# Four units' first halves ahead of the shift, and the shift's last tile multiplied by TensorE, in a two-block kernel on one core

## The chip, the cores and the metric

One core of a Trainium2 chip runs the whole program in one launch. The metric is the device time of one execution in microseconds. Engines are called TensorE (PE in the profile), its weight loads (PEld), VectorE (DVE), ScalarE (ACT), GpSimd (POOL) and SyncE (SP), which issues all loads.

## The reference, cut to what matters

Two blocks are computed over 512 tokens of width 1024 (8 tiles of 128 channels). The part around the change is the beginning of the first block:

```
mod = silu(c) @ w_cond[l] + b_cond[l]
shift_m, scale_m, gate_m, shift_f, scale_f, gate_f = split(mod, 6)
h = rmsnorm(x, g_mix_pre[l]) * (1.0 + scale_m) + shift_m
q, k, v, u = split(h @ w_in[l], ...)
attn = stick_breaking_attention(q, k, v)      # 8 heads of 64
mix = concat([attn, pooling_mixer(u)]) @ w_out[l]
x = x + gate_m * rmsnorm(mix, g_mix_post[l])
```

A gated feed-forward (2816 wide) follows, then the second block with a chunked state-space mixer, a short convolution and another feed-forward. All results are float32.

## The kernel before, in words

**Layout.** Channels lie on the 128 partitions, tokens along the row, so each activation is 8 tiles of 128x512. A weight matrix is cut into units: one unit is a 128-column strip of the output with all 8 tiles of the contraction, 128x1024 float32. SyncE loads it into a ring of four `raw` buffers. ScalarE rounds it to `whi` (`hi`, L1075), GpSimd writes the rest `wlo = raw - whi` (`lo`, L489; in quarters for the first three units), and activations are split in the same way. A unit is three products for each of 8 tiles, high x high, high x low and low x high: 24 matmuls of 512 columns (`unit`, L549, L550, L553).

**Counters.** The order on each engine is written out by hand; engines wait for counting semaphores. SyncE's queue is one order for all loads: a load whose ring slot is taken holds up all behind it.

**The conditioning.** `mod` is a product with a vector. Its weights come as 48 tiles of 128x1024, `cond`, in a ring of four. VectorE multiplies each by its factor and adds it to `macc` (`mod_unit`, L1610 for the first of eight, L1613 for the others); TensorE then sums `macc` over the partitions with one-column matmuls (`mod_first`, L606; `mod_sum`, L598 for the later parts). Two tiles of the scale (8 and 9) are multiplied by TensorE itself (`mod_direct`, L615). Tiles 0 to 7 are the shift, 8 to 15 the scale of the first norm.

**The start.** SyncE loads x, then the 16 tiles, then units 0 to 3. ScalarE squares x (L1082), TensorE sums the squares (L584), ScalarE makes the root. VectorE multiplies x by it (`norm_x`, L1544) between its conditioning tiles. When shift and scale are both there (`mod_ready` 2), VectorE and ScalarE write the high part `h1h` (L1550, L1128), ScalarE the whole (L1134), VectorE the low part `h1l` (L1554). `first_pair` multiplies units q0 and k0 side by side (L625, L628, L632, L637), then follows v0.

**The heads.** Units come in the order q0 k0 v0 q1 k1 v1 u0 q2 k2 v2 u1 q3 k3 v3 u2 u3. For each head TensorE makes the scores (`scores`, L681); VectorE masks them (L1651), ScalarE and VectorE make a soft-plus (L1195 to L1204, L1661, L1665), TensorE adds the later keys (`later_keys`, L691, L695), ScalarE makes weights (L1211), TensorE the product with the values (`values`, L707). `BETWEEN` says which units stand before and behind the later keys of each head. In every head but the last VectorE adds four more conditioning tiles, and the low parts of q and k (`qk_low`, L1704).

**The output and the joints.** `out_first` is the first output unit; the last conditioning part is summed (`mod_sum(5)`), and three more units follow. Then pieces are handled in halves of 256 tokens: ScalarE squares and copies each output piece (`out_piece`, L1253, L1254), VectorE adds the squares and, once the root is there, the residual (`half_x`, L1595, L1590), ScalarE squares the new x (`x_squares`, L1108), TensorE sums those squares between its strips (`x_sum`, L576, placed by `SUMS_OUT`), ScalarE makes the root (`x_rms`) and h2 is formed (`half_h`, L1566, L1578; `split_half`, L1122). The joint between the blocks is built in the same way, with `down_piece` and h3.

## Time and profile before

| | us |
|---|---|
| median of 3 runs | 1733.77 (1731.59 to 1736.16) |
| the profiled execution | 1734.22 |
| its span | 1732.4 |
| TensorE busy | 1692.5 (98%) |
| TensorE's weight loads | 1377.0 (79%) |
| GpSimd busy | 785.0 (45%) |
| VectorE busy | 734.0 (42%) |
| ScalarE busy | 707.8 (41%) |

The span is that of the profiled execution, from its first to its last instruction; 1.8 us lie around it. The mean granted clock of TensorE is 0.989 of full speed. A share is an average over the span: it doesn't tell which engine ends last in a stage. The chain that ended last is TensorE for 92%, VectorE for 4%, loads and ScalarE for 1% each.

### The profile page before, as it was taken

The numbers are of one execution on the slowest core, as the hardware profiler recorded it, in microseconds if no ns is written. First come the engines' busy times: TensorE is split into PE (matmuls) and PEld (weight loads), VectorE is DVE, ScalarE is ACT, GpSimd is POOL, SyncE is SP. The second block draws the span as 40 slices with busy tenths as digits, with TensorE's granted clock in tenths as the row PEclk, the third lists the DMA queues.
The fourth block names the chain that finished last, engine by engine and source line by source line (L and its number), as shares of the span: only waits on it lengthen the run. The fifth ranks groups of instructions, "written<-read, shape, count | busy, mean of one in ns | idle before, by whom it ended". The sixth has DMA issues, their size and how long they took to land.

```text
span 1732.4 us, 22044 instructions
## 1 busy us (share of the span) xinstructions
PE 1692.5 (98%) x8046; PEld 1377.0 (79%) x8046; DVE 734.0 (42%) x1120; ACT 707.8 (41%) x952; POOL 785.0 (45%) x612
## 2 busy tenths in 40 slices
PE   4999999999999999999999999999999999999998
PEld 3777698888888889888888888887888788888887
DVE  4576825111110026567768778676013222222002
ACT  2655536222223345433534545445223544333232
POOL 0533234444446653543434434445444444444763
PEclk8999999999999999999999999999999999999999
DMA  8544312322323323332332232322333222332332
GB/s 314 190 151 157 123 64 71 116 89 97 97 74 87 96 85 122 123 109 86 101 106 99 96 110 94 101 86 85 98 100 132 96 87 95 97 97 72 93 91 73
DMA packets 54132, 184.61 MB, mean 107 GB/s; under 512 B 5904, under 2 KB 8208, under 8 KB 53680
## 3 DMA queue, kind: packets, MB, share of 16 engines
q1 hardware_dynamic: 54064, 183.67, 32.2%
q8 instruction: 46, 0.75, 0.2%
q14 instruction: 22, 0.18, 0.0%
HBM read 179.39 MB, written 4.26 MB: 106 GB/s over the span
## 4 chain that ended last, share of the span: by engine, by line
PE 92%; DVE 4%; ACT 1%; DMA 1%; issue 1%; SPq 0%; DVEq 0%; ACTq 0%
PE PR L549 26%; PE PR L550 26%; PE PR L553 26%; PE PR L563 2%; PE PR L564 2%; PE PR L565 2%; PE AX L947 1%; DMA cond<-wcond 1%; DVE macc L1613 1%; PE AX L681 1%; PE AX L951 1%; PE AX L707 1%; PE AX L936 1%; PE AX L576 1%; PE AX L691 1%
## 5 line engine op out<-in xcount | busy, mean ns | idle before, releaser
L489 POOL TENSOR_TENSOR wlo<-raw,whi 128x512 fp32r<-128x512 f32 (+1 forms) x600 | 778.8, 1322 | 895.9 <-ACT whi L1075 895.9
L1075 ACT ACTIVATE whi<-raw 128x1024 fp32r<-128x1024 f32 x288 | 301.6, 1051 | 151.5 <-PE PR L553 132.4
L549 PE MATMUL PR<-h3h,whi 128*128 128x512 f32 x608 | 245.5, 404 | 0.0
L550 PE MATMUL PR<-h3l,whi 128*128 128x512 f32 x608 | 240.4, 395 | 0.0
L553 PE MATMUL PR<-h3h,wlo 128*128 128x512 f32 x608 | 154.1, 395 | 0.0
L549 PE MATMUL PR<-h4h,whi 128*128 128x512 f32 x351 | 139.4, 397 | 0.0
L550 PE MATMUL PR<-h4l,whi 128*128 128x512 f32 x351 | 138.6, 395 | 0.0
L553 PEld LDWEIGHTS PR<-h3h,wlo 128*128 128x128 f32 x608 | 114.2, 188 | 27.6
L549 PEld LDWEIGHTS PR<-h3h,whi 128*128 128x128 f32 x608 | 114.3, 188 | 26.7 <-issue 1.2
L550 PEld LDWEIGHTS PR<-h3l,whi 128*128 128x128 f32 x608 | 114.4, 188 | 26.4 <-issue 1.0
L549 PE MATMUL PR<-h2h,whi 128*128 128x512 f32 x320 | 126.7, 396 | 0.0
L550 PE MATMUL PR<-h2l,whi 128*128 128x512 f32 x320 | 126.4, 395 | 0.0
L549 PE MATMUL PR<-fh,whi 128*128 128x512 f32 x308 | 121.9, 396 | 0.0
L550 PE MATMUL PR<-fl,whi 128*128 128x512 f32 x308 | 121.7, 395 | 0.0
L1304 ACT ACTIVATE fh<-ff 128x512 f32 (+1 forms) x44 | 27.8, 632 | 197.0 <-DVE ff L1791 98.5
L1781 DVE TENSOR_TENSOR ff<-sg,PR 128x512 f32<-128x512 f32 x22 | 15.2, 689 | 182.3 <-PE PR L553 175.2
L553 PE MATMUL PR<-h4h,wlo 128*128 128x512 f32 x351 | 89.1, 396 | 0.0
L553 PE MATMUL PR<-h2h,wlo 128*128 128x512 f32 x320 | 81.2, 396 | 0.0
L553 PE MATMUL PR<-fh,wlo 128*128 128x512 f32 x308 | 81.0, 396 | 0.0
L549 PEld LDWEIGHTS PR<-h4h,whi 128*128 128x128 f32 x351 | 65.9, 188 | 16.4 <-issue 0.2
L550 PEld LDWEIGHTS PR<-h4l,whi 128*128 128x128 f32 x351 | 66.0, 188 | 15.9 <-issue 0.2
L553 PEld LDWEIGHTS PR<-h4h,wlo 128*128 128x128 f32 x351 | 65.9, 188 | 16.0
(328 smaller groups left out, 2981.7 us busy)
## 6 DMA issues: line engine op xcount, KB each, us to landing
raw<-w SPq DMA_DIRECT2D x224, 512.0 KB, 3.5
cond<-wcond SPq DMA_DIRECT2D x48, 512.0 KB, 4.6
raw<-w SPq DMA_DIRECT2D x32, 384.0 KB, 3.1
raw<-w SPq DMA_DIRECT2D x32, 320.0 KB, 2.9
abc_a<-acum_rows SPq DMA_DIRECT2D x8, 512.0 KB, 4.0
abc_b<-acum_rows SPq DMA_DIRECT2D x8, 512.0 KB, 4.4
x<-xin SPq DMA_DIRECT2D x1, 2048.0 KB, 10.3
x_keep<-x SPq DMA_DIRECT2D x1, 2048.0 KB, 7.3
```

What stands on the lines that cost most here:

```text
L489: ins = pool.tensor_tensor(wlo[:, j, a:a + n], raw[:, j, a:a + n], whi[:, j, a:a + n], ALU.subtract)
L549: pe.matmul(bank, whi[:, j, w], oh[:, k0 + k, :], start=first and i == 0, stop=False)
L550: pe.matmul(bank, whi[:, j, w], ol[:, k0 + k, :], start=False, stop=False)
L553: mm = pe.matmul(bank, wlo[:, j, k * P:(k + 1) * P], oh[:, k0 + k, :], start=False, stop=last and i == n - 1)
L563: pe.matmul(bank[:, c], whi[:, j, w], oh[:, k0 + k, c], start=start, stop=False)
L564: pe.matmul(bank[:, c], whi[:, j, w], ol[:, k0 + k, c], start=False, stop=False)
L565: return pe.matmul(bank[:, c], wlo[:, j, w], oh[:, k0 + k, c], start=False, stop=stop)
L576: mm = pe.matmul(AX[:, 3, HALF[q % 2]], con_("ones"), sqx[:, k, :], start=k == 0, stop=k == KT - 1)
L681: mm = pe.matmul(AXf[:, c:c + T - j * P], ks[r, p % 2, j * P:(j + 1) * P], qs[r, p % 2, j * P:T], start=j != 3 and i == 0, stop=False, ski ...
L691: mm = pe.matmul(AXf[:, c:c + T - j * P], late[:, 2, :], part[:, c:c + T - j * P], start=False, stop=part is spl and j == NCH - 1, skip_gr ...
L1075: act.activation(whi[:, j, :], raw[:, j, :], ACT.Copy).then_inc(hi_ready, 1)
L1304: act.activation(tile(fh, 2 * i + b), ff[:, b, :], ACT.Copy).then_inc(fh_ready, 1)
```

## The change

The first norm's product is split in two: first x times its root and its scale, `xa` (held in `mixh`, `mixl`), without the shift. Units 0 to 3 (q0, k0, v0, q1) are multiplied with `xa`; what the shift adds to them is a constant for each output channel. It is made apart: the shift in a high and a low part is the stationary operand (two columns, `shifts`), the weights of two units are the moving one (256 columns), which gives two rows (`shift_rows`); two tiny matmuls turn them into columns (`shift_columns`), and VectorE and ScalarE add these when they read q0, k0, v0 and q1. Unit 4 (k1) and all later ones use the whole h1, with the shift (`first_whole`).

The scale is loaded and added ahead of the shift, in two halves of four output tiles (pairs of half-wide tiles, `load_scale`, `mod_scale`). After the first half come the first four tiles of `xa` and the first halves (tiles 0 to 3) of units 0 to 3; after the second half come tiles 4 to 7. x is loaded in two pieces, and squared into buffers of its own. The loads of units 0 to 3 stand between those of the scale, ahead of the shift. The shift's tiles come last; of its eight, VectorE adds seven and TensorE multiplies the last by itself (`mod_direct(KT - 1)`).

k1 moves ahead of the scores of head 0, and q1 too; heads 0 and 1 keep one unit each. `mod_sum(5)` moves behind the second output unit. At the joints, squares of x stand ahead of an output piece on ScalarE and VectorE, and `SUMS_OUT` sums them earlier. Buffers are placed anew (h1l beside, `shifts` and `bias` added).

```
-FIRST_COND = (0, 1, 2, 3, 4, 5, 8, 6, 9, 7, 10, 11, 12, 13, 14, 15)
-DIRECT = (8, 9)
-BETWEEN = [("q1", "k1"), ("v1", "u0"), ("q2", "k2"), ("v2", "u1"), ("q3", "k3"), ("v3",), ("u2",), ("u3",)]
+EARLY = 4
+BETWEEN = [("v1",), ("u0",), ("q2", "k2"), ("v2", "u1"), ("q3", "k3"), ("v3",), ("u2",), ("u3",)]
...
-SUMS_OUT = {(1, 7): (0, 1), (2, 2): (2,), (2, 5): (3,), (2, 7): (4,), (3, 0): (5,), (3, 1): (6,), (3, 2): (7,)}
+SUMS_OUT = {(1, 7): (0, 1), (2, 2): (2,), (2, 4): (3,), (2, 5): (4,), (2, 6): (5,), (2, 7): (6,), (3, 0): (7,)}
...
+            def load_scale(e, i):
+
+                at = RING * e + i
+                j = at % RING
+                if at >= RING:
+                    sp.wait_ge(cond_used, at - RING + 1)
+                src = wcond[KT + 2 * i:KT + 2 * i + 2, :, 512 * e:512 * e + 512].rearrange("a p n -> p a n")
+                sp.dma_start(cond[:, j, :].rearrange("p (a n) -> p a n", a=2), src).then_inc(cond_in[j], 16)
...
+            sp.dma_start(x[:, 0:4, :], xin[:, 0:4, :]).then_inc(s_x[0], 16)
+            sp.dma_start(x[:, 4:KT, :], xin[:, 4:KT, :]).then_inc(s_x[1], 16)
+            for i in range(4):
+                load_scale(0, i)
+            load_in(0)
+            load_in(1)
+            for i in range(4):
+                load_scale(1, i)
+            load_in(2)
+            load_in(3)
+            for n in range(KT):
+                load_cond(KT + n, n)
             sp.dma_start(att[:, :, :], atts[:, :, :]).then_inc(s_att, 16)
...
+            def sumsq(ks):
+
+                for k in ks:
+                    pe.wait_ge(sq_ready, k + 1)
+                    mm = pe.matmul(AX[:, 0, :], con_("ones"), mix1[:, k, :], start=k == 0, stop=k == KT - 1)
+                mm.then_inc(sq_used, 1)
...
+            def early_first():
+
+                for u in range(2):
+                    pe.wait_ge(hi_ready, u + 1)
+                    for k in range(4):
+                        pe.wait_ge(*xa_high(k))
+                        early(u, whi, mixh, k, start=k == 0)
+                for k in range(4):
+                    pe.wait_ge(xa_low, k + 1)
+                    for u in range(2):
+                        early(u, whi, mixl, k)
+                for u in range(2):
+                    pe.wait_ge(lo_ready, u + 1)
+                    for k in range(4):
...
+            def early_unit(u, ks, between=None):
+
+                pe.wait_ge(hi_ready, u + 1)
+                for k in ks:
+                    early(u, whi, mixh, k, start=k == 0)
+                    early(u, whi, mixl, k)
+                if between is not None:
+                    between()
+                pe.wait_ge(lo_ready, u + 1)
+                for k in ks:
+                    early(u, wlo, mixh, k, stop=k == KT - 1)
...
+                    for part in (whi, wlo):
+                        mm = pe.matmul(AX[0:2, 3 - u // 2 * 2, 0:2 * P], shifts[:, k, :], part[:, u:u + 2, k * P:(k + 1) * P],
+                                       start=k == 0 and part is whi, stop=k == KT - 1 and part is wlo,
+                                       skip_group_check=True)
+                mm.then_inc(unit_used, 2)
...
+            sumsq(range(KT))
+            mod_part(1, range(4), 4)
+            early_first()
+            early_unit(2, range(4))
+            early_unit(3, range(4), between=lambda: mod_part(1, range(4, KT), 8))
+            early_second()
+            mod_direct(KT - 1)
+            early_unit(2, range(4, KT))
+            early_unit(3, range(4, KT), between=lambda: mod_part(0, range(KT), 15))
+            shift_rows(0)
+            shift_rows(2)
+            shift_columns(0)
...
+            def first_whole(u):
+
+                pe.wait_ge(hi_ready, u + 1)
+                for k in range(KT):
+                    if k == 4:
+                        shift_columns(2)
...
             out_first()
-            mod_sum(5)
             for m in range(1, 4):
                 if m == 2:
+                    mod_sum(5)
                     pe.wait_ge(pooll_ready, 4)
                 if m == 3:
-                    pe.wait_ge(mod_ready, 3)
+                    pe.wait_ge(mod_ready, 4)
...
+            rms(1, sq_used, 1, dst=AX[:, 1, :])
+            act.wait_ge(mod_ready, 1)
+            xa(0)
             hi(0, 4, 0)
+            xa(2)
             hi(0, 4, 1)
+            for k in range(4):
+                xa_whole(k)
+            hi(0, 4, 2)
+            hi(0, 4, 3)
             act.wait_ge(mod_ready, 2)
-            for k in range(KT // 2, KT):
+            for k in range(4, KT):
+                xa(k)
+            for k in range(4, KT):
+                xa_whole(k)
+            act.wait_ge(mod_ready, 3)
+            act.activation(shifts[:, :, 0], mod[:, 0:KT], ACT.Copy).then_inc(shift_ready, 1)
+            for k in range(6):
                 h1_high(k)
-            for k in range(4):
-                full(k)
-            hi(0, 4, 2)
-            for k in range(4, KT):
-                full(k)
+            hi(0, 4, 4)
+            h1_high(6)
...
+            act.wait_ge(bias_ready, 2)
+            act.activation(kh[:, 0, :], PR[:, 1, :], ACT.Identity, bias=bias[:, 1:2]).then_inc(qkvu_ready, 1)
+            for p in range(2):
+                act.wait_ge(q_whole, p + 1)
+                act.activation(qh[:, p, :], pw[:, p * T:(p + 1) * T], ACT.Copy).then_inc(qkvu_ready, 1)
+            act.wait_ge(bias_ready, 4)
+            act.activation(vT[:, :], PR[:, 2, :], ACT.Identity, bias=bias[:, 2:3]).then_inc(qkvu_ready, 1)
+            hi(0, 4, 5)
             act.wait_ge(s_att, 16)
             act.activation(late[:, :, :], att[:, :, :], ACT.Copy).then_inc(late_ready, 1)
-            for u in range(3):
-                in_step(u)
+            hi(0, 4, 6)
+            in_step(4)
...
-            x_squares(0, (3, 4, 5))
-            out_piece(10)
-            x_squares(0, (6, 7))
+            x_squares(0, range(3, KT))
             hi(0, 4, U_GU1 + 2)
             x_rms(0)
-            split_half(0, h2h, (0, 1), shift1)
+            split_half(0, h2h, (0,), shift1)
+            out_piece(10)
+            split_half(0, h2h, (1,), shift1)
...
-            x_squares(2, (5,))
+            x_squares(2, (5, 6, 7))
             down_piece(8)
-            x_squares(2, (6, 7))
...
+            for i in range(4):
+                mod_scale(0, i)
+            dve.wait_ge(s_x[0], 16)
             dve.wait_ge(r_ready, 1)
...
+            for k in range(4):
+                norm_x(k)
+            scale(0)
+            dve.wait_ge(mod_ready, 1)
+            xa(1)
+            xa(3)
+            for k in range(4):
+                xa_lower(k)
+            for i in range(4):
+                mod_scale(1, i)
+            dve.wait_ge(s_x[1], 16)
+            norm_x(4)
+            scale(1)
+            for k in range(5, KT):
+                norm_x(k)
             dve.wait_ge(mod_ready, 2)
-            make_h()
+            mod_unit(KT)
+            for k in range(4, KT):
+                xa_lower(k)
+            for n in range(1, KT - 1):
+                mod_unit(KT + n)
+            dve.wait_ge(msum_done, 3)
+            dve.tensor_scalar(mod[:, 0:KT], PR[:, 3, 0:KT], 1.0, None, ALU.mult).then_inc(mod_ready, 1)
+            dve.wait_ge(shift_ready, 1)
+            dve.wait_ge(mod_ready, 3)
+            dve.tensor_tensor(shifts[:, :, 1], mod[:, 0:KT], shifts[:, :, 0], ALU.subtract).then_inc(shift_ready, 1)
+
...
+            for k in range(3):
+                h1_lower(k)
+            rows(0)
+            h1_lower(3)
+            h1_lower(4)
+            rows(2)
+            h1_lower(5)
+            columns(0)
+            whole_q(0)
+            h1_lower(6)
+            h1_lower(7)
+            dve.wait_ge(qkvu_ready, 1)
+            dve.scalar_tensor_tensor(kl[:, 0, :], PR[:, 1, :], bias[:, 1:2], kh[:, 0, :], ALU.add,
+                                     ALU.subtract).then_inc(qkl_ready, 1)
+            columns(2)
+            whole_q(1)
+            whole_q_low(0)
+            whole_q_low(1)
...
-            half_x(2, mix2, gffn, lambda k: down_piece(8) if k == 6 else None)
+            half_x(2, mix2, gffn)
+            down_piece(8)
```

`load_cond` and `mod_unit` now count by the position in the ring; a tile's load waits until the tile four places before it is taken.

## Rows read from the trace of the kernel before

**Rows 1.** Waits of TensorE over the whole run: line, releaser: us in total, times, longest.

```profile
PE PR L606 <- DVE macc L1613: 9.8, 2, 9.0
...
PE PR L563 <- DVE h2l L1578: 1.3, 2, 0.9
```

**Rows 2.** Timeline of TensorE at the start: start, us, line, count, idle before and releaser.

```profile
12.75 9.29 PE L584 MATMUL AX<-sq,con 128*128 128x512 f32 x16 [7.46 <-ACT sq L1082]
...
21.95 1.95 PE L615 MATMUL PR<-cvec,cond 128*128 128x1 f32 x16
...
40.18 3.57 PE L606 MATMUL PR<-con,macc 128*128 128x1 f32 x16 [8.99 <-DVE macc L1613]
...
45.26 6.38 PE L625 MATMUL PR<-h1h,whi 128*128 128x512 f32 x16 [1.50 <-DVE h1h L1550]
...
64.64 0.44 PE L681 MATMUL AX<-qh,kh 64*128 64x384 f32 x1
```

**Rows 3.** Windows: busy us of each engine, granted clock, DMA share, GB/s.

```profile
10.00:15.00 5.00, 2.25 (x3) 1.18 (x4) 1.29 (x2) 1.31 (x3) 0.00 (x0) 1.00 0.94 386
...
26.00:27.00 1.00, 0.85 (x8) 0.76 (x7) 0.72 (x1) 0.00 (x0) 0.00 (x0) 0.83 0.84 303
...
50.00:51.00 1.00, 1.00 (x4) 0.73 (x3) 0.55 (x1) 1.00 (x2) 0.15 (x1) 0.72 0.00 0
...
218.00:220.00 2.00, 2.00 (x8) 1.81 (x8) 0.68 (x2) 0.00 (x0) 0.00 (x0) 0.50 0.15 59
```

**Rows 4.** The chain that ended last: start, us, engine and line.

```profile
62.84 1.87 PE PR L553 x8
...
83.45 2.30 PE AX L707 x8
...
221.91 0.43 PE PR L549
```

**Rows 5.** Timeline of VectorE, ScalarE and GpSimd at the start.

```profile
13.32 0.75 DVE L1610 TENSOR_SCALAR macc<-cond,cvec 128x1024 f32<-128x1024 f32 x1 [12.09 <-DMA cond<-wcond]
14.46 5.45 DVE L1613 SCALAR_TENSOR_TENSOR macc<-cond,cvec,macc 128x1024 f32<-128x1024 f32 x4 [0.39 <-DMA cond<-wcond]
...
32.87 1.28 DVE L1544 TENSOR_TENSOR xn<-x,AX 128x512 f32<-128x512 f32 x2
...
38.66 1.06 ACT L1075 ACTIVATE whi<-raw 128x1024 fp32r<-128x1024 f32 x1 [15.21 <-DMA raw<-w]
...
39.79 5.91 POOL L489 TENSOR_TENSOR wlo<-raw,whi 128x256 fp32r<-128x256 f32 x8 [39.34 <-ACT whi L1075]
...
44.07 2.93 ACT L1128 ACTIVATE h1h<-xn,mod,amix 128x512 fp32r<-128x512 f32 x4 [3.07 <-DVE amix L1637]
...
50.85 7.20 POOL L489 TENSOR_TENSOR wlo<-raw,whi 128x256 fp32r<-128x256 f32 x6 [5.15 <-ACT whi L1075]
...
51.51 4.13 DVE L1554 TENSOR_TENSOR h1l<-xn,h1h 128x512 fp32r<-128x512 f32 x4 [0.97 <-ACT xn L1134]
```

**Rows 6.** The conditioning tiles' own view, 0 to 60 us.

```profile
DMA to landing us min/median/max: 4.1/5.1/13.3
```

**Rows 7.** Timeline of VectorE in heads 0 to 2.

```profile
82.01 0.69 DVE L1704 SCALAR_TENSOR_TENSOR kl<-PR,kh 128x512 fp32r<-128x512 f32 x1 [1.08 <-ACT kh L1168]
...
90.09 8.20 DVE L1613 SCALAR_TENSOR_TENSOR macc<-cond,cvec,macc 128x1024 f32<-128x1024 f32 x4
101.36 0.99 DVE L1651 TENSOR_TENSOR AX<-AX,att 128x128 f32<-128x128 f32 x3 [3.07 <-PE AX L681]
```

**Rows 8.** Timeline of TensorE and ScalarE around the last conditioning sum.

```profile
216.63 2.52 PE L598 MATMUL PR<-con,macc 128*128 128x1 f32 x16 [1.61 <-DVE macc L1613]
...
227.43 0.60 ACT L1253 ACTIVATE sq<-PR 128x512 f32<-128x512 f32 x1 [5.40 <-PE PR L553]
```

**Rows 9.** Timeline of TensorE at the joint of the blocks.

```profile
641.84 2.75 PE L576 MATMUL AX<-sqx,con 128*128 128x256 f32 x12
645.33 1.13 PE L576 MATMUL AX<-sqx,con 128*128 128x256 f32 x4 [0.74 <-ACT sqx L1108]
```

More of the change, by code:

```diff
@@ L578, in x_sum @@
                     mm.then_inc(sqx_done, 1)
-            def sumsq(first):
-                for k in range(KT):
-                    pe.wait_ge(sq_ready, first + k + 1)
-                    mm = pe.matmul(AX[:, 0, :], con_("ones"), sq[:, k % 2, :], start=k == 0, stop=k == KT - 1)
-                    mm.then_inc(sq_used, 1)
+            def sumsq(ks):
[3 more added lines that the diff above has]
+                mm.then_inc(sq_used, 1)
             def sum_once(n):
@@ new lines, in early_second @@
+            def early_second():
+                for k in range(4, KT):
+                    pe.wait_ge(*xa_high(k))
+                    for u in range(2):
+                        early(u, whi, mixh, k)
+                for u in range(2):
+                    for k in range(4, KT):
+                        early(u, wlo, mixh, k)
+                for k in range(4, KT):
+                    pe.wait_ge(xa_low, k + 1)
+                    for u in range(2):
+                        early(u, whi, mixl, k, stop=k == KT - 1)
@@ L641, in _, with shift_columns @@
+            def shift_columns(u):
+                pe.wait_ge(rows_taken, u // 2 + 1)
+                for n in (u, u + 1):
+                    mm = pe.matmul(AX[:, u // 2 * 3, n:n + 1], pooled[0:2, n * P:(n + 1) * P], con_("ones", 0, 1, rows=2), start=True,
+                                   stop=True, skip_group_check=True)
+                mm.then_inc(bias_done, 1)
             pe.wait_ge(s_vec, 16)
```

267 lines of the change are left out of this document (140 added, 127 removed).

## The prediction

> **What bounds the kernel.** I read the page first: TensorE is busy 98% of the span and the chain that ended last is 92% TensorE. From its first dense matmul on, time can only come from its idle stretches and from stretches at half clock. So I went to the list of its waits: 9.8 us stand at the start and 1.3 at the first joint between blocks, both at places that the change touches [rows 1]. The timeline of the start shows the reader why: the sum of squares is over at 22.0, the first dense matmul comes at 45.26, the scores of head 0 at 64.64 [rows 2]. Before 45.26 the kernel waits for loads, then for VectorE, which adds the conditioning tiles. The granted clock was 1.00 during the sum of squares, fell inside 26 to 27 and came back inside 50 to 51, 5 us after the first dense matmul [rows 3]. A matmul of 512 columns takes 0.234 us at the upper level (1.87 for eight) and 0.43 at the lower [rows 4]; a unit (24 of them) is 5.6 us.
>
> Two units more are moved ahead of the scores (q1, k1 beside q0, k0, v0), so the start breaks even if the scores begin at 64.6 + 11.2 = 75.9. All times of the new order are my estimates, worked out from rows.
>
> **The start, step by step.** (a) Loads: from the first conditioning tile (13.32) to the first weight unit, sixteen transfers later (38.66), each half megabyte took 1.58 us [rows 5]. The new order puts four half-width scale pairs first: the fourth lands at 18.0, or 18.3 with some 0.1 each for rows half as long (bounds 0 and 0.5). VectorE adds a full tile in 1.36 (5.45 for four) [rows 5]; two half-wide operations I put at 1.5: done at 19.9. Four norm products at 0.64 and the small factors: 22.6. ScalarE's first scaled tile (0.73) and first high weight part (1.0) follow [rows 5]: TensorE starts its first dense matmul at 24.3, 21 us earlier than now. The sum of squares, which starts with the first half of x, is over by 16 and is hidden.
>
> (b) Up to the sum of the second half of the scale TensorE has 44 matmuls. It starts at the lower clock: ten at 0.43 and 34 at 0.234 make 12.4, so 36.7 if nothing waits. But VectorE and GpSimd now work side by side: four low parts and eight half-wide adds against the low weight parts. Where they did so before, a 512-wide VectorE operation took 1.03 (4.13 for four) instead of 0.69 [rows 7], and a quarter of a low weight part 1.2 (7.20 for six) instead of 0.74 (5.91 for eight) [rows 5]. With 1.1 for both, unit 1's low part is ready at 33.4 and unit 2's at 37.5; TensorE waits 2.3 and 1.3 there and reaches the sum at 40.4. It is over at 41.4, and VectorE, idle since 36.7 behind that wait, has the second half of the factors at 41.6.
>
> (c) Behind it in VectorE's queue stand three norm products, the first shift tile, four low parts and three more shift tiles: 1.9 + 0.75 + 2.6 + 3 x 1.38 = 9.4, so 51.0. Only then is the ring slot free for the last shift tile, the one that TensorE multiplies itself; SyncE waits for it there, with the loads of units 4 to 7 queued behind (needed only from 70 on: hidden). The shortest landing of such a tile was 4.1 us [rows 6]: it is there at 55.0.
>
> (d) TensorE finishes what it has (28 matmuls, with short waits for the high parts) at 48.7 and idles 6.3 us, since the multiplication stands ahead of the rest in its queue. Before, the clock fell 5 us after the last dense matmul, in spite of one-column matmuls [rows 2, 3]; so I take it as lower from some 53 on.
>
> (e) From 55.0: sixteen one-column matmuls, 3.57 at the lower clock (1.95 at the upper) [rows 2]; twelve dense at 0.43: 63.7; eight at 0.234, sixteen one-column, four dense: 68.5. The row product of the shift is new: 32 matmuls of 256 columns. No row shows one with two output rows; the nearest bounds are a one-column matmul, 0.12 (1.95 for sixteen), and a 512-column one, 0.234: 3.8 or 7.5. I take 3.8, half the columns of the latter. 72.4. Then unit 4 (5.6), two column turns (1.0), waits for ScalarE's high and GpSimd's low part (1.3), and VectorE's corrected q (0.9): the scores start at 81.2. Against 75.9 the start **costs 5.3**: 21 us of lead are spent on waits and half clock. Bounds: -5 (no gap, no lower clock: 10.2 less) and +9.
>
> **Heads 0 and 1** lose a unit of TensorE work each, 11.2 us; VectorE's conditioning tiles there stay. It had 1.1 and 3.1 us idle and drops one low part (0.7) [rows 7]: 6.3 us of debt. The four tiles of head 1 took 8.20, against 5.45 for four without GpSimd beside them [rows 5, 7], and GpSimd now has one unit less there: up to 2.8 comes back. TensorE asks for the result only behind the values product (2.30) [rows 4]. 6.3 - 2.8 - 2.3: I take **+1.0**, bounds 0 and 6.3.
>
> **The sum of the last conditioning part** is moved behind unit 1 of the output. Now TensorE waits 1.61 for it (from 215.0), then sums at falling clock, and unit 1 is over only at 227.4; the clock was 0.50 in 218 to 220 [rows 3, 8]. 12.4 us for 5.6 + 1.95: moved, the tile is there before it is asked for, and 4.9 return. Units 2 and 3 wait for nothing longer than their own work: **-4.9**, bounds -1.6 and -4.9.
>
> **Joints.** In the first, the squares no longer stand behind an output piece: the first product of h2 had waited 0.9 (1.3 in two waits) [rows 1]: **-1.1**, bounds 0 and -1.3. What is late next there is the piece that was put back; it is due with unit 2 of the next stage, and has 0.4 us. In the second, the last two squares came 0.74 after the six before were summed (641.84 + 2.75 = 644.6; 645.33) [rows 9]; that is on the way to h3, for which TensorE stands idle: **-0.8**, bounds 0 and -1.2. Changed tables, buffers and semaphores cost nothing.
>
> Sum: +5.3 + 1.0 - 4.9 - 1.1 - 0.8 = -0.5. The profiled execution took 1734.22 (span 1732.4): 1733.7. It stands 0.45 above the median of 1733.77, so the forecast for the median is **1733.3**. Some 0.3% (5.2 us) is what a measurement of this kernel can tell from no change.
>
> **A rule weighed.** The Trainium skill (SBUF — State Buffer, section on its two separate sides) calls the port pair of VectorE and GpSimd an exclusive lock: the loser fully blocks for the whole instruction. The measured pairs [rows 5, 7] speak against full exclusion: 0.69 + 0.74 would be 1.43 per pair, and 1.03 to 1.2 was measured. By rows alone, full exclusion would lengthen twelve VectorE operations by 0.33 each: 4.0 later, 1737.3. By that rule this is what to expect.
>
> **Rivals.**
> 1. Forecast, 1733.3: chance 0.45.
> 2. The clock stays up through the gap, or comes back at once: 1.6 + 2.3 less, 1729.4. For: it was up during the idle first 12 us. Against: 26 to 27 [rows 3]. 0.15.
> 3. The gap closes: VectorE is quicker in (b) and (c), the last tile lands before 48.7. 10.2 less: 1723.1. For: (c) hangs on one wait of VectorE, and every us that TensorE gains in (b) is gained twice. Against: 4.1 us of landing behind 9.4 of VectorE. 0.12.
> 4. **Slower:** VectorE becomes the bound of heads 0 to 2. Place: the later keys of heads 1 and 2, which need its low part. Price: the debt of 6.3 in full, 5.3 more: 1738.6. It decides from the point where the four tiles keep their 8.20 and the low part comes more than 2.3 late. For: VectorE worked without a pause between heads there except for 1.1 and 3.1. 0.12.
> 5. Full exclusion of the two engines: 1737.3, 0.08.
> 6. The late sum does not do what it should: the clock falls behind unit 1 instead, or the tile is still late: 1738.2, 0.08. Against: sums of the same kind stand between dense work elsewhere without a wait.
>
> Each case carries some 4 us of its own from the unknown prices. Below 1728.6 lie case 3, almost half of 2 and a tail of 1: 0.26. Above 1739 lie half of 4 and parts of 1, 5 and 6: 0.16. The range of 8 in 10: **1725 to 1740**.
>
> **What would show it.** Right: first dense matmul near 24; TensorE waiting for the last shift tile's load some 6 us and the clock at 0.50 behind it; scores of head 0 at 81; VectorE waiting 4 to 5 us for the column sums of the second half scale; no wait and no half clock around the late sum; no wait over 0.3 at h2. Wrong: scores near 76 or earlier (cases 2, 3); low parts of weights ready as fast as alone (b); waits of the later-keys product in heads 1 and 2 above 2 us (case 4). If the start is right and the median is still below 1728, a stage behind the joints changed that I took as equal.

## The result, and the profile of the changed kernel

The changed kernel took 1738.86 us (median of 7 runs, 1736.63 to 1739.41), beside 1734.82 for the kernel before on the same chip (7 runs). The ratio is 1.0024, with an interval of 1.0015 to 1.0034: **slower by 4.1 us**. The forecast was "the same, 1733.3". The median lies inside the range of 1725 to 1740, but the change did something that can be measured, and it went the other way from the forecast. The rivals that end slower (4, 5 and 6) had 0.28 between them, and 0.16 stood for a time above 1739.

The profiled execution has a span of 1736.5 us, against 1732.4 before: the same 4.1. So the trace can be read as a ledger. First the waits of TensorE over the whole run (line, releaser: us in total, times, longest):

```profile
PE PR L626 <- DMA cond<-wcond: 8.9, 1, 8.9
...
PE PR L632 <- ACT whi L1156: 4.7, 1, 4.7
...
PE PR L632 <- POOL wlo L501: 2.5, 1, 2.5
...
PE PR L575 <- DVE h2l L1666: 1.0, 2, 0.6
```

Before, 9.8 us stood before the column sums and 1.3 at h2l [rows 1]. The largest wait is now on a load, in front of the direct multiplication, and it comes in the middle of dense work. TensorE's timeline of the start:

```profile
18.98 1.05 PE L618 MATMUL PR<-con,macc 128*128 128x1 f32 x8
24.72 3.55 PE L632 MATMUL PR<-mixh,whi 128*128 128x512 f32 x8 [4.69 <-ACT whi L1156]
...
33.58 1.19 PE L632 MATMUL PR<-mixh,wlo 128*128 128x512 f32 x4 [2.51 <-POOL wlo L501]
...
40.82 0.95 PE L618 MATMUL PR<-con,macc 128*128 128x1 f32 x8
...
47.05 2.03 PE L632 MATMUL PR<-mixl,whi 128*128 128x512 f32 x8
57.96 3.57 PE L626 MATMUL PR<-cvec,cond 128*128 128x1 f32 x16 [8.88 <-DMA cond<-wcond]
...
67.96 1.84 PE L618 MATMUL PR<-con,macc 128*128 128x1 f32 x16
70.66 0.28 PE L681 MATMUL AX<-whi,shifts 128*2 128x256 f32 x1
...
83.43 0.41 PE L763 MATMUL AX<-qh,kh 64*128 64x384 f32 x1 [0.93 <-ACT late L1330]
```

It is the order that the forecast had, step for step; the scores of head 0 come at 83.43 instead of 64.64 [rows 2], and with two units (11.2) paid off, the start costs 7.6. Why the load came so late is in the timelines of VectorE, GpSimd and SyncE's queue:

```profile
28.41 7.95 DVE L1718 SCALAR_TENSOR_TENSOR macc<-cond,cvec,macc 128x512 f32<-128x512 f32 x7
36.28 0.67 DVE L1730 TENSOR_TENSOR xn<-x,AX 128x512 f32<-128x512 f32 x1
41.80 0.16 DVE L1725 SCALAR_TENSOR_TENSOR amix<-PR,vec 128x4 f32<-128x4 f32 x1 [4.85 <-PE PR L618]
41.88 1.87 DVE L1730 TENSOR_TENSOR xn<-x,AX 128x512 f32<-128x512 f32 x3
43.67 0.75 DVE L1697 TENSOR_SCALAR macc<-cond,cvec 128x1024 f32<-128x1024 f32 x1
44.34 2.74 DVE L1740 SCALAR_TENSOR_TENSOR mixl<-xn,amix,mixh 128x512 fp32r<-128x512 f32 x4
46.99 6.84 DVE L1700 SCALAR_TENSOR_TENSOR macc<-cond,cvec,macc 128x1024 f32<-128x1024 f32 x5
...
24.75 15.38 POOL L501 TENSOR_TENSOR wlo<-raw,whi 128x256 fp32r<-128x256 f32 x14 [24.30 <-ACT whi L1156]
...
29.55 21.85 SPq L389 DMA_DIRECT2D cond<-wcond  x8
51.45 0.43 SPq L434 DMA_DIRECT2D att<-atts  x1
```

SyncE began the issue of the eighth shift tile at 51.1, when VectorE had emptied the slot, and ended it at 51.4; TensorE went on at 57.96. Counted as in [rows 6], from the start of the issue to the landing, the three last shift tiles took (the tiles' own view, 48 to 55 us):

```profile
L389 SPq DMA_DIRECT2D cond<-wcond x3: 328/328/328, 48.3 to 51.1; - x3
DMA to landing us min/median/max: 3.4/4.7/6.8
```

They were issued 1.4 us apart and landed in their order, after 3.4, 4.7 and 6.8 us. VectorE idles for 4.85 us, from 36.9 to 41.8, waiting for the column sum, at a time when the first two shift tiles already lie in the ring: they landed at 32.9 and 35.3. That line turned out to be the most useful one of the trace.

The granted clock, in windows (busy us of PE, PEld, VectorE, ScalarE, GpSimd, then the clock, DMA share, GB/s):

```profile
36.00:37.00 1.00, 1.00 (x4) 0.80 (x3) 0.95 (x2) 0.00 (x0) 1.00 (x2) 0.50 0.88 360
...
64.00:65.00 1.00, 1.00 (x4) 0.71 (x4) 0.00 (x0) 0.00 (x0) 0.00 (x0) 0.50 1.01 414
87.00:88.00 1.00, 1.00 (x4) 0.81 (x3) 0.00 (x0) 0.97 (x2) 1.00 (x2) 0.50 0.94 340
203.00:204.00 1.00, 1.00 (x3) 0.26 (x2) 0.97 (x5) 0.00 (x0) 0.00 (x0) 0.50 1.02 418
230.00:232.00 2.00, 2.00 (x18) 1.90 (x16) 0.00 (x0) 0.00 (x0) 0.00 (x0) 1.00 0.00 0
```

It is at the lower level (1.2 GHz, 0.50) in 21.0 to 27.9 and in 51.8 to 65.4, as forecast, and in three short stretches that were not: 34.7 to 38.1, 85.9 to 89.3 and 201.9 to 205.4. Around the late sum it is 1.00, where it had been 0.50 before [rows 3].

At the very start the windows mislead. The trace has no record of the clock before 14.2 us here and before 16.4 in the kernel before, and a window without a record prints 1.00. The matmuls of the sum of squares tell more: here they start 0.86 us apart from 10.6 to 14.0 and 0.43 apart from 14.5 on, in the kernel before 0.86 apart from 13.7 to 16.3. So TensorE's first work ran at half the pace of what followed, and the reading "1.00 during the sum of squares" [rows 3] holds only for its second part. That the clock was up in the idle first 12 us, as case 2 of the prediction has it, no row shows.

The ledger, by how much later each point comes than before, the two units taken off up to head 1: scores of head 0, +7.6; scores of heads 3 to 5, +9.4; pool map behind head 7 and first output unit, +10.0; first piece behind the late sum, +5.0; first h2 product, +4.8; first gate of the next stage, +5.1; end, +4.1. So: start +7.6, heads +2.4, tail -5.0, joint 1 nothing, joint 2 -1.0.

### The profile page after: what moved, and what is told of

Same layout as the page of the kernel before. It is cut to its first block, busy times and chain, and to the rows that moved or that the text cites. A ratio compares the mean times of both kernels' runs of the same rounds, so it can differ in the third digit from the quotient of the medians.

```text
span 1736.5 us, 22124 instructions
## 1 busy us (share of the span) xinstructions
PE 1697.9 (98%) x8070; PEld 1378.5 (79%) x8070; DVE 746.5 (43%) x1145; ACT 712.3 (41%) x963; POOL 786.6 (45%) x612
## 3 DMA queue, kind: packets, MB, share of 16 engines
q1 hardware_dynamic: 55232, 183.67, 32.9%
## 4 chain that ended last, share of the span: by engine, by line
PE 94%; DVE 3%; ACT 1%; DMA 1%; issue 0%; POOL 0%; SPq 0%; DVEq 0%; POOLq 0%; ACTq 0%
PE PR L561 26%; PE PR L562 26%; PE PR L565 26%; PE PR L575 2%; PE PR L576 2%; PE PR L577 2%; PE AX L1028 1%; PE AX L789 1%; PE AX L763 1%; PE AX L1032 1%; PE AX L773 1%; PE AX L588 1%; PE PR L632 1%; PE AX L777 1%; PE AX L596 1%; PE AX L1017 1%
## 5 line engine op out<-in xcount | busy, mean ns | idle before, releaser
L561 PEld LDWEIGHTS PR<-h4h,whi 128*128 128x128 f32 x351 | 65.9, 188 | 16.4 <-issue 0.2
```

The source lines that it names most:

```text
L561: pe.matmul(bank, whi[:, j, w], oh[:, k0 + k, :], start=first and i == 0, stop=False)
```

## The experiments

All ratios are against the kernel before, which ran beside each group; the changed kernel stands at 1.0024. Where a gain is given in us of time, it is worked out from the ratios. The groups ran on different chips, so a difference of two ratios carries some 2.3 us of doubt: e2, e4 and e6 lie within it or near its edge, and the others that are set against the changed kernel are clear of it. "Head 0" and "head 3" are the starts of these heads' scores: 83.43 and 128.34 in the changed kernel, 64.64 and 118.98 before.

**e1: the direct multiplication behind units 2 and 3.**

```
             early_second()
-            mod_direct(KT - 1)
             early_unit(2, range(4, KT))
-            early_unit(3, range(4, KT), between=lambda: mod_part(0, range(KT), 15))
+            early_unit(3, range(4, KT))
+            mod_direct(KT - 1)
+            mod_part(0, range(KT), 15)
```

> The changed kernel, with the multiplication of the last shift tile moved on TensorE behind the second halves of units 2 and 3 (24 matmuls). Theory S (the loss at the start is TensorE's: it stands at the last tile, 49.0 to 58.0, with 24 matmuls queued behind that need no tile, and does half of them at the lower clock afterwards): the 24 are done at 54.6, the wait shrinks to 3.4 us, scores of head 0 at 76 to 78.5 instead of 83.4, whole time 5 to 7 us below the changed kernel. Rival R (VectorE is the bound of heads 0 to 2 and takes back what the start saves): scores of head 0 as early, but those of head 3 at most 2 us earlier than in the changed kernel (128.4), whole time 0 to 2 us below it.

Ratio 1.0002 (0.9993 to 1.0012): 3.8 us come back, the whole loss. Timeline of TensorE:

```profile
55.76 2.33 PE L626 MATMUL PR<-cvec,cond 128*128 128x1 f32 x16 [1.84 <-DMA cond<-wcond]
57.95 3.55 PE L618 MATMUL PR<-con,macc 128*128 128x1 f32 x16
```

The wait fell from 8.88 to 1.84, head 0 to 76.33, head 3 to 121.22 (7.1 earlier). So the rival fell, since head 3 came earlier by as much as head 0; but the time gained is less than the theory's 5 to 7. Behind head 3 this trace has three stretches of lower clock (166.4, 197.1 and 647.7), the changed kernel's has one. The same work was only put in another order: what cost was a wait with 5.6 us of ready work queued behind it.

**e2: the last tile's load with nothing behind it** (SyncE waits for its landing before it issues the next loads).

```
+            sp.wait_ge(cond_in[RING - 1], 64)
             sp.dma_start(att[:, :, :], atts[:, :, :]).then_inc(s_att, 16)
```

> The changed kernel, with all loads behind the last shift tile held back until that tile has landed. Theory S (the tile landed 7 us after its issue at 51 instead of 4.1, because ten loads issued right behind it share the engines): it lands by 55.5, scores of head 0 at 81, whole time 2 to 3 us below the changed kernel. Rival L (7 us is what a tile costs there, whoever else loads): it lands near 58 again, the time is the same within 0.5 us.

Ratio 1.0017 (1.0007 to 1.0026), head 0 at 82.41. From the start of its issue the tile took 6.1 us to land with no load behind it, while the kernels that kept the loads there (e6, e1, e3, e4, e7 and the changed one) gave 5.1, 5.4, 5.7, 5.7, 6.4 and 6.8. The loads queued behind are not what makes it late: the theory fell. Two things are left open. One is scatter: e4 has the same start as the changed kernel, to the instruction, and its tile took 5.7. The other is what stands in front: in e2 too the two tiles before it, issued 1.4 us apart, took 3.4 and 4.4. Whether the last one queues behind those, no run here tests.

**e3: the gap filled with dense work** (32 matmuls of 512 columns into a bank that nobody reads, ahead of the direct multiplication; they add nothing to the result).

```
             early_second()
+            for k in range(32):
+                pe.matmul(AX[:, 0, :], whi[:, 0, 0:P], mixh[:, k % KT, :], start=True, stop=True, skip_group_check=True)
             mod_direct(KT - 1)
```

> The changed kernel, with 32 dense matmuls into an unused bank put ahead of the multiplication of the last shift tile: they fill 7.5 us of the 8.9 us in which TensorE stood idle, and compute nothing that is used. Theory S (the clock falls in the gap and costs 3.9 us behind it: sixteen one-column matmuls at 3.6 instead of 2.0, twelve dense at 0.43 instead of 0.234): granted clock 1.00 from 50 to 70, scores of head 0 at 79.5, whole time 3.5 to 5.5 us below the changed kernel. Rival C (the clock there costs nothing, since the shift waits for VectorE anyway): the same within 0.5 us.

Ratio 0.9997 (0.9987 to 1.0006): 4.7 us under the changed kernel with more work done. In its trace:

```profile
49.62 7.63 PE L705 MATMUL AX<-mixh,whi 128*128 128x512 f32 x32
57.51 1.95 PE L626 MATMUL PR<-cvec,cond 128*128 128x1 f32 x16 [0.27 <-DMA cond<-wcond]
```

The direct multiplication is back at its 1.95 [rows 2]; the clock stayed at 1.00 until 59.5, then was low for 3.4 us instead of 13.6. Head 0 came at 81.08, where the theory had 79.5: the profiled execution gained only 2.4 us at heads 0 and 3; the ratio gained more. So the gap has two prices: 8.9 us of standing, and a clock that stays low for 7.5 us after it.

**e4: the late sum put back ahead of unit 1.**

```
             out_first()
+            mod_sum(5)
             for m in range(1, 4):
                 if m == 2:
-                    mod_sum(5)
```

> The changed kernel with the last conditioning sum back ahead of the second output unit, as before. Theory S (moving it returned 5.1 us: end of the output unit after it 10.0 us late against before on one side, 4.9 on the other): 4 to 5.5 us above the changed kernel, TensorE waits 1.6 us for VectorE there and the clock falls behind it. Rival T (the gain at that place came from the shifted phase of the work around it, not from the move): within 1.5 us of the changed kernel.

Ratio 1.0040 (1.0027 to 1.0054): 2.8 us more than the changed kernel, less than expected. The profile shows the wait of 1.63 again; the clock did fall, at 227.9 to 231.3, but for 3.4 us instead of 6.8 before (217.8 to 224.6). (The expectation of e9 below says that it did not fall here; that is wrong.)

**e5: VectorE takes the last shift tile.**

```
-            mod_direct(KT - 1)
...
-            early_unit(3, range(4, KT), between=lambda: mod_part(0, range(KT), 15))
+            early_unit(3, range(4, KT), between=lambda: mod_part(0, range(KT), 16))
...
-            for n in range(1, KT - 1):
+            for n in range(1, KT):
```

> VectorE takes the last shift tile as it takes the others, and TensorE's own multiplication of it is gone; the column sum of the shift stays where it is, between the two passes of unit 3. Theory (what costs is the place of TensorE's wait, not who multiplies): the tile lands at 56 to 58, VectorE needs 1.0 to 1.4 us for it, TensorE has meanwhile done the second half of unit 2 and the first pass of unit 3, the sum starts at 57.5 to 59.5 instead of 67.96, and the scores of head 0 come at 74 to 77 instead of 83.4; the time is 3.5 to 5.5 us under the changed kernel's. Rival (TensorE's multiplication itself saves something that VectorE then has to pay): scores of head 0 above 79 and less than 2.5 us gained.

Ratio 0.9989 (0.9979 to 0.9999), 6 us under the changed kernel, a little more than expected, though head 0 at 77.7 is later than the theory's 77. Timelines of VectorE and TensorE:

```profile
58.14 1.28 DVE L1699 SCALAR_TENSOR_TENSOR macc<-cond,cvec,macc 128x1024 f32<-128x1024 f32 x1 [1.48 <-DMA cond<-wcond]
...
59.48 3.57 PE L618 MATMUL PR<-con,macc 128*128 128x1 f32 x16 [4.87 <-DVE macc L1699]
```

This undoes the part of the change that its short description names. The tile landed just as late (58.1), VectorE added it in 1.28, and TensorE had by then done the 4.7 us of work that it otherwise left behind its wait.

**e6: the scale's second column sum 2.9 us earlier** (between the passes of unit 2 instead of unit 3).

```
-            early_unit(2, range(4))
-            early_unit(3, range(4), between=lambda: mod_part(1, range(4, KT), 8))
+            early_unit(2, range(4), between=lambda: mod_part(1, range(4, KT), 8))
+            early_unit(3, range(4))
```

> Only the second half of the scale's column sum moves on TensorE, from between the passes of unit 3 to between those of unit 2, about 2.9 us earlier (VectorE has its operand ready at about 36.3). Theory (the last shift tile waits for its slot, the slot for VectorE, and VectorE for this sum): VectorE's idle stretch of 4.85 us shrinks to 2 to 2.5, the slot comes free 2.5 to 3 us earlier, the direct multiplication starts at 54.5 to 55.5, scores of head 0 at 80 to 81.5, and the time falls by 2 to 3 us against the changed kernel. Rival (the landing is set by the transfers, not by the slot): direct multiplication still at 56.5 or later, time within 1 us of the changed kernel.

Ratio 1.0011 (1.0001 to 1.0020), 2.3 us gained. VectorE's idle stretch fell to 2.08, the direct multiplication came at 53.59, head 0 at 79.72. The direct multiplication came 4.4 earlier: the slot was free 2.7 earlier, as the theory had it, and the other 1.7 are a landing of 5.1 us instead of 6.8.

**e7: VectorE's idle stretch filled.**

```
-            norm_x(4)
-            scale(1)
-            for k in range(5, KT):
+            for k in range(4, KT):
                 norm_x(k)
-            dve.wait_ge(mod_ready, 2)
             mod_unit(KT)
+            mod_unit(KT + 1)
+            scale(1)
+            dve.wait_ge(mod_ready, 2)
+            mod_unit(KT + 2)
+            mod_unit(KT + 3)
             for k in range(4, KT):
                 xa_lower(k)
-            for n in range(1, KT - 1):
+            for n in range(4, KT - 1):
```

> VectorE alone is reordered: the last three normalizations and the first two shift tiles fill its idle stretch ahead of the scale's factors, and the third and fourth shift tile go ahead of the low parts. Theory: VectorE is busy from 36.3 to about 41, frees the slot of the last shift tile at 44.5 to 45.5 instead of 50.6, the tile lands at 49.5 to 51.5, TensorE's idle stretch behind the first two units shrinks from 8.9 us to 0.5 to 2.5, scores of head 0 at 76 to 78.5, the time 4.5 to 7 us under the changed kernel's. Rival (the shift tiles have not landed by 41, or land 7 us after their slot whatever is done): idle stretch above 4 us, time less than 3.5 us under.

Ratio 0.9987 (0.9978 to 0.9997), 6.4 us gained. Timelines of SyncE's queue and of TensorE:

```profile
29.49 15.30 SPq L389 DMA_DIRECT2D cond<-wcond  x8
44.84 0.43 SPq L434 DMA_DIRECT2D att<-atts  x1
...
50.91 2.31 PE L626 MATMUL PR<-cvec,cond 128*128 128x1 f32 x16 [2.08 <-DMA cond<-wcond]
```

The eighth tile was issued at 44.8 instead of 51.4, and head 0 and head 3 moved by 7.4 each. Nothing was taken away; VectorE only did ready work while it waited: its next conditioning tile begins at 38.6 instead of 43.7.

**e8: e7, and the direct multiplication between units 2 and 3.**

```
-            mod_direct(KT - 1)
             early_unit(2, range(4, KT))
-            early_unit(3, range(4, KT), between=lambda: mod_part(0, range(KT), 15))
+            mod_direct(KT - 1)
+            mod_part(0, range(KT), 15)
+            early_unit(3, range(4, KT))
```

> VectorE as in the run before this one, and on TensorE the direct multiplication and the shift's column sum stand between the second halves of unit 2 and unit 3, so that unit 3 covers what the other engines do with the sum. Theory: no wait above 1 us at the direct multiplication, which starts at 51 to 53; shift rows done at 60 to 63; scores of head 0 at 69.5 to 73 instead of 83.4; 8 to 12 us under the changed kernel, 1727 to 1731, so 4 to 8 us under the kernel before. Rival (VectorE then bounds the first heads, and gives back what came earlier): scores of head 0 as said, but head 3 less than 7 us earlier than in the changed kernel, and less than 5 us gained in time.

Ratio 0.9962 (0.9950 to 0.9975): 10.8 us under the changed kernel and 6.6 under the one before. No wait is left at the direct multiplication (52.90). Head 0 at 73.05, head 3 at 119.18, 9.2 earlier: the next heads gave back 1.2. The trace shows a stretch of lower clock at 74.3 to 81.1 that takes 3.1 up to head 1, of which 1.2 are left at head 3.

**e9 and e12: the old start.** e9 is the kernel before with only `mod_sum(5)` moved as in the change; e12 also has the new `SUMS_OUT` and the new orders of squares and pieces at both joints, so that only the start is the old one.

Of e9:

> The kernel before with one edit of the change: the last column sum behind the heads, mod_sum(5), stands behind unit 1 of the output projection instead of ahead of it. The prediction priced this at -4.9 us; putting it back in the changed kernel cost only 2.8 us by the medians (1.5 of it in the profiled execution, whose clock did not fall). Theory (its worth is the wait of 1.6 us plus the stretch of lower clock that follows a wait with one-column matmuls): 3 to 5 us under the kernel before, ratio 0.997 to 0.998, no granted clock of 0.50 between 217 and 224 us. Rival (only the wait itself, 1.6 us; the lower clock comes anyway): ratio about 0.999, clock still 0.50 for 4 us or more.

Of e12:

> The kernel before with all of the change but its start: the late sum of the run before this one, and the new orders of squares, sums and pieces at both joints. The new start is then what is missing. Theory (the joints give 0.3 us at the first and 1.0 at the second): 1.0 to 1.5 us under the run with the late sum only, 4.5 to 6.5 us under the kernel before. Rival (the joints give nothing that reaches the end): within 0.5 us of the late sum alone. The changed kernel is 4.1 us slower than the kernel before, so by the theory its start costs 9 to 10 us of time.

Ratios 0.9981 (0.9972 to 0.9990) and 0.9975 (0.9966 to 0.9983): -3.3 and -4.3 us. In e9 the sum runs without a wait at full clock:

```profile
221.48 1.84 PE L598 MATMUL PR<-con,macc 128*128 128x1 f32 x16
```

The joints seem worth 1.0 more, but the two intervals overlap, so the times alone don't show it. The traces do show where it would lie: at the first joint the wait for h2 is 0.3 shorter in e12, and from the first h2 product to the gate it takes 27.2 us where e9 has 26.9, so nothing is left; at the second, from the first sum of squares to the first h3 product, it takes 6.2 instead of 7.2. Against e12 the changed kernel's start, with the heads behind it, costs 0.49%, 8.5 us of time.

**e10 and e11.** e10 is e8 with ScalarE's `late` between its two copies of q; e11 is e10 with `hi(0, 4, U_GU1 + 2)` behind `x_rms(0)` and the first tile of h2h.

Of e10:

> VectorE's filled idle stretch and the direct multiplication between units 2 and 3, as in the best run so far, and ScalarE makes the tile late in the gap between the two copies of q instead of behind the fifth copy of a weight tile. TensorE waited 1.35 us for late at 71.7. Theory: scores of head 0 at 71.0 to 72.2 instead of 73.05, and the time 1 to 1.5 us under that run; if the stretch of lower clock at 74.6 to 80.9 was set off by that wait, it goes too and another 2 to 3 us with it. Rival (VectorE's chain of the scale-shifted low parts, or the first softmax, is next in line): scores 1 us earlier, head 1 unchanged at 87, time unchanged.

Of e11:

> The run before this one, and at the first joint ScalarE copies the high part of unit U_GU1+2 behind the inverse norm and the first tile of h2h instead of ahead of them, so that GpSimd's low part of that unit no longer runs beside VectorE's first low part of h2 (1.08 us there against 0.65 in the kernel before and 0.47 alone). Theory: that VectorE instruction takes 0.5 to 0.7 us, TensorE's wait for it falls from 0.64 to 0.1 to 0.3 us, time 0.3 to 0.5 us lower, too little for the median to show. Rival (the low part of the weight now comes late): a wait of TensorE for wlo of 1 us or more behind the joint, time 0.5 to 2 us higher.

e10: 0.9960 (0.9944 to 0.9976), not to be told from e8. TensorE's wait for `late` is gone, and so is the stretch of lower clock at 74.3; head 0 comes at 72.42 and head 1 at 83.96 (87.11 in e8). That isn't the work of the edit: e13 below is e8 once more, keeps the wait of 1.35 and has no such stretch, and its heads 0, 1 and 3 come at 73.03, 83.99 and 117.92, those of e10 at 72.42, 83.96 and 118.18. So the rival held: scores 0.6 earlier, and nothing left of it at head 1. In e10 a new stretch of lower clock follows at 123.1 to 126.5. e11: 0.9977 (0.9966 to 0.9988), a miss. VectorE's first low part is as short as expected, but the rival came true in full:

```profile
263.39 0.55 PE L575 MATMUL PR<-h2h,whi 128*128 128x256 f32 x1 [2.95 <-POOL wlo L501]
```

The low part of that weight unit was due right there: 0.6 us saved, 2.95 lost, and the clock fell behind it.

**e13, e14 and e15, on one chip.** e13 is e8 once more, e14 is e12 once more. e15 is e8 without the direct multiplication: VectorE takes the last tile, and the column sum of the shift stands between the passes of unit 3, as in e5.

Of e13:

> The kernel with VectorE's stretch filled and the direct multiplication between units 2 and 3, once more, beside the next two on one chip. Theory (the changed kernel's start is worth more than the old one once its two waits are gone): ratio to the kernel before 0.995 to 0.997, and 1 to 3 us under the old start with the new tail. Rival (the repaired start is worth just what the old one is, and the gain is the tail's and the joints' alone): within 1 us of the old start with the new tail.

Of e14:

> The kernel before with the late sum and the new joints, once more. Theory: 0.997 to 0.998 of the kernel before, 1 to 3 us above the run before this one. Rival: equal to it within 1 us.

Of e15:

> As the first of these three, but VectorE takes the last shift tile too, and TensorE's direct multiplication (1.7 us) is gone; the column sum stands between the two passes of unit 3. Theory (the tile lands at about 51, VectorE is done with it at 53.5 to 54.5, TensorE reaches the sum at 54 to 55): no wait above 0.5 us at the sum, shift rows within 1 us of the first run's, scores of head 0 at 72 to 73.5, time within 1 us of the first run: who multiplies is then worth nothing. Rival (with the waits gone TensorE's 1.7 us is what counts): scores of head 0 at 71 to 71.7, time 1 to 2 us lower.

e13: 0.9956 (0.9942 to 0.9970), 1727.3 us. e14: 0.9972 (0.9962 to 0.9982), 1730.1. So the repaired start looks some 2.8 us better than the old one, but the intervals overlap, so it isn't shown; both comparisons (e8 with e12, e13 with e14) lean the same way. **e15: 0.9944 (0.9930 to 0.9958), 1725.6 us, the lowest time: 9.7 us under the kernel before by the ratio (8.1 by the medians), beside it on one chip, and some 14 under the changed one.** Its interval overlaps that of e13. Timeline of TensorE:

```profile
53.31 1.84 PE L618 MATMUL PR<-con,macc 128*128 128x1 f32 x16
55.01 1.16 PE L632 MATMUL AX<-mixh,wlo 128*128 128x512 f32 x4
...
68.78 0.41 PE L762 MATMUL AX<-qh,kh 64*128 64x384 f32 x1 [0.92 <-ACT late L1329]
```

A window of e15, just behind the column sum:

```profile
56.00:57.00 1.00, 1.00 (x10) 0.72 (x9) 0.76 (x2) 1.00 (x3) 0.00 (x0) 1.00 1.04 426
```

Head 0 comes 4.3 us earlier than in e13, more than the theory and the rival had: 1.7 for the sixteen matmuls that are gone, 1.4 because this execution ran that much earlier before the edited place (the last pass of unit 2 at 50.51 instead of 51.91), and the rest from the clock. The time leans to the rival: 1.7 us under e13 by the medians, where it had 1 to 2. In e13, sixteen and then sixteen one-column matmuls run back to back (52.84 to 56.3) and the clock is 0.50 behind them, in this window of e13:

```profile
57.00:58.00 1.00, 1.00 (x3) 0.72 (x3) 0.56 (x2) 1.00 (x2) 0.00 (x0) 0.50 1.03 422
```

In e15 sixteen stand alone between dense passes, and it stays at 1.00 (2.4 GHz) in every window from 29 to 310 us.

## Why the prediction was wrong, point by point

**(a), right in the sum.** First dense matmul forecast at 24.3, measured 24.72. Two sizes inside it were off and cancelled: VectorE had its eight half-wide operations done at 18.9 instead of 19.9, and the sum of squares was over at 19.0 instead of 16, its first part at half the pace, so that VectorE idled 1.5 us for the root.

**(b), right in the sum, in part by luck.** Column sum over at 41.4 by the forecast, 41.8 in the trace. The first of the two forecast waits came (2.3 forecast, 2.51 measured). The second, 1.3, did not: eight matmuls ran at 0.43 instead of 0.234 in its place (34.7 to 38.1), which took 1.5. In e15 the clock stayed up there, and the wait is there with 1.05. A half-wide add took 1.14 beside GpSimd (7.95 for seven) and a quarter of a low part 1.10 (15.38 for fourteen); 1.1 was assumed for both. By the Trainium skill (SBUF — State Buffer, section on its two separate sides) the two lock each other out. The sum of the two alone (0.81, from 5.68 for the first seven half-wide adds, and 0.74) would be 1.5 per pair, and the trace again shows less.

**(c), its last term was mis-sized.** VectorE frees the slot at 51, as forecast. Then I took the shortest landing of the kernel before, 4.1 us, although the same row gave a median of 5.1 [rows 6]. The changed kernel's profile has 6.8, e1 to e7 have 5.1 to 6.4: the median too would have been at the low end. Forecast 55.0, measured 57.96: three microseconds, and TensorE stood still for all of them. This is the step that made the start +7.6 instead of +5.3 (0.7 of the three came back behind it). Part of it may be one execution's scatter (5.7 in e4, with the same start); what makes this tile slower than those before it stays open.

**(d), (e), right.** TensorE done at 49.0 (48.7), lower clock from 51.8 (53), the direct multiplication 3.57, shift rows 0.117 each (0.12). From the landing to the scores 26.2 were forecast, 25.5 measured.

**Heads: +1.0 forecast, +2.4 measured: the debt was under-sized, and it is not the lower clock.** From the scores of head 0 to those of head 3 the changed kernel takes 44.9 us. So do e1 to e7, e13 and e15, those with a stretch of lower clock near head 0 (the changed kernel, e3, e5) and those without: heads 0 to 1 take 12.5 us in the first and 11.0 in the others, and by head 3 nothing is left of that. The kernel before takes 54.3, less two units 43.1. So +1.8 belongs to the new order. It is VectorE's: it masks the scores of head 1 3.4 us after they began (95.95), those of head 2 4.8 us after (108.85), and comes to both masks straight from the tiles and low part below, without a pause. Before, it masked them 1.5 us after and had idled 3.07 for those of head 2 [rows 7].

```profile
93.06 5.78 DVE L1700 SCALAR_TENSOR_TENSOR macc<-cond,cvec,macc 128x1024 f32<-128x1024 f32 x3
98.75 0.68 DVE L1893 SCALAR_TENSOR_TENSOR kl<-PR,kh 128x512 fp32r<-128x512 f32 x1
99.35 0.82 DVE L1840 TENSOR_TENSOR AX<-AX,att 128x128 f32<-128x128 f32 x3
...
106.64 7.13 DVE L1700 SCALAR_TENSOR_TENSOR macc<-cond,cvec,macc 128x1024 f32<-128x1024 f32 x4
113.69 0.82 DVE L1840 TENSOR_TENSOR AX<-AX,att 128x128 f32<-128x128 f32 x3
```

In e4, without that stretch of lower clock, TensorE's later keys wait for the soft-plus that comes of it:

```profile
103.61 0.45 PE L773 MATMUL AX<-sph,late 128*128 128x384 f32 x1 [0.53 <-ACT sph L1299]
```

So case 4's mechanism did occur, at 1.8 us instead of its 6.3; of the 2.8 that I let come back through GpSimd, the four tiles of head 1 gave 1.1 (7.13 instead of 8.20). No run took work off VectorE in the heads, so this rests on the traces alone. That the median of 1738.86 stands at case 4's 1738.6 is chance. The other 0.7 came behind head 3: the stretch of lower clock at 201.9 takes 1.7, and a wait of 0.95 for the pooled values that TensorE had before is gone. No term of the sum stood for it.

**Tail: -4.9 forecast, -5.0 in the profile, -3.3 in time** (e9) and -2.8 (e4). The working holds for the profiled execution, whose clock fell behind the wait; over many executions it seems not to fall always or not for as long, and then only the wait of 1.6 is saved. That average was not traced; it is inferred from e4 and e9.

**Joint 1: -1.1 forecast, nothing measured.** The step "what is late next there is the piece that was put back" failed. The norm did come 0.7 earlier against the end of the dense strip, but VectorE's first low part now ran beside GpSimd's next weight part, and two pieces' sums (L1937) stand between the first low parts, where it was one:

```profile
269.70 1.08 DVE L1666 SCALAR_TENSOR_TENSOR h2l<-hth,mod,h2h 128x256 fp32r<-128x256 f32 x1 [0.19 <-ACT h2h L1210]
270.71 0.41 DVE L1937 TENSOR_TENSOR ssum<-ssum,sq 128x256 f32<-128x256 f32 x1
271.05 0.47 DVE L1654 SCALAR_TENSOR_TENSOR hth<-x,affn,AX 128x256 f32<-128x256 f32 x1
```

The first wait fell from 0.90 to 0.64, and the half behind it grew by 0.3. **Joint 2: -0.8 forecast, -1.0 measured**; the sixteen sums run in one piece:

```profile
646.91 3.62 PE L588 MATMUL AX<-sqx,con 128*128 128x256 f32 x16
```

**The sign.** Three errors of +2.3 (the landing), +1.4 (the heads) and +1.1 (joint 1) all went the same way. The range bore that, the chances did not: the cases that end slower were each one mechanism in full, and little was left for several terms of my own forecast being each a little short. The clue for what would have helped was in the forecast: case 3, "the gap closes", hung on one wait of VectorE. It was priced as luck; e7 shows that it was a matter of order.

## What to carry to other kernels

A wait on a late load belongs behind all work that is ready, and an engine that idles for a result should do whatever has landed: two reorderings without new work turned +4.1 us into -6.6 (e8; the tail and joint 2 are part of that), and giving the last tile back to VectorE leans further the same way (-9.7, with intervals that overlap). Splitting a stage to start early pays only so far as the ring behind it is emptied early as well: look at which slot the last load waits for, then at what that slot's reader is idle for. Price a landing from tiles that are issued in the same way, not at the best of all: the last of three issued 1.4 us apart took 6.8 us, the first 3.4. Price each long wait of TensorE twice: the wait and the half clock behind it.

## What the hardware showed that I had not expected

In e15 sixteen one-column matmuls between dense passes left the clock at 1.00 (53.3), and so did those of the late sum (230.5 in the changed kernel); thirty-two in a row (e13), or sixteen behind a wait (of 1.6 us at 216.6 in the kernel before, of 2.1 in e7, of 4.9 in e5), were followed by 0.50. But sixteen without a wait can be followed by it too: the stretch at 201.9 of the changed kernel stands right behind such a sum (200.03 to 201.9), and those at 123.1 in e10 and 193.7 in e8 begin 1.9 and 2.8 us after the start of one; in e13 and e15 the same sums are followed by nothing. In the same way a wait of 2.5 us (for the low part of unit 1, ending at 33.6) was followed by 3.4 us of lower clock in the changed kernel, and the same wait of 2.3 in e15 was not. Each short stretch takes 1.5 to 1.7 us where it stands, which is as much as some of the effects that were looked for here; what is left of it further on depends on who bounds the next stage (nothing at head 3 for the one at 85.9, 0.7 for the one at 201.9). What decides whether the clock falls at such a place is open.
